# Forgetting attention's last gate products spread over the following units, its pooling splits moved behind them, and a cross-attention norm's sums moved to TensorE

## The reference, cut to what matters

```
z = rms_norm(x, mix_pre_g) @ w_in        # pool, q, k, v, forget logits, two gates of 1024 columns
y_pool = pool_mixer(u_pool, ...) @ w_pool_br
y_fox  = fox_attention(q, k, v, log_f) @ w_fox_br     # 8 heads, 8 query blocks of 128, causal
merged = sigmoid(z_gp) * y_pool + sigmoid(z_gf) * y_fox
x = x + rms_norm(merged @ w_mix_out, mix_post_g)
x = x + rms_norm(mem_attention(rms_norm(x, xa_pre_g), ...), xa_post_g)
h = rms_norm(x, ffn_pre_g)
x = x + rms_norm(conv_ffn(h, ...), ffn_post_g)
```

## Time and profile before

| what | us |
|---|---|
| median of 3 runs | 2921.78 (2920.51 to 2922.21) |
| the profiled execution, its own time | 2927.9 |
| its span, first to last instruction | 2926.0 |
| TensorE busy in it | 2823.0 (96%) |
| VectorE busy | 1270.6 (43%) |
| ScalarE busy | 795.1 (27%) |
| mean granted clock of TensorE | 0.984 |

### The profile page before, as it was taken

One profiled execution on the slowest core, in us unless ns is written; L12 is line 12 of the kernel. 1 busy time (PEld: TensorE's weight loads), 2 busy tenths in 40 slices (PEclk: granted clock), 3 DMA queues, 4 the chain that ended last, 5 costly groups with the idle time before them and its releaser, 6 DMA issues.

```text
span 2926.0 us, 35159 instructions
## 1 busy us (share of the span) xinstructions
PE 2823.0 (96%) x13916; PEld 2307.3 (79%) x13916; DVE 1270.6 (43%) x1788; ACT 795.1 (27%) x1234; POOL 970.0 (33%) x1008
## 2 busy tenths in 40 slices
PE   7999988999999999999999998999979999999998
PEld 6889876888888888878797776777658888888886
DVE  4266636543323223255204343458476343433436
ACT  5254426220001101143113333334452111111114
POOL 3622310743333333324332110364125333333330
PEclk9999999999999999999999999999989999999999
DMA  5423331311111111116543232432012111111103
GB/s 206 157 100 101 101 123 40 119 52 63 43 46 54 43 43 57 35 23 134 131 94 91 80 108 85 169 115 87 29 72 72 56 45 43 43 43 43 66 20 115
DMA packets 156934, 230.59 MB, mean 79 GB/s; under 512 B 5285, under 2 KB 116240, under 8 KB 156824
## 3 DMA queue, kind: packets, MB, share of 16 engines
q1 hardware_dynamic: 110448, 136.85, 16.2%
q10 hardware_dynamic: 46375, 92.24, 9.0%
HBM read 181.33 MB, written 47.74 MB: 78 GB/s over the span
## 4 chain that ended last, share of the span: by engine, by line
PE 84%; DVE 9%; ACT 3%; issue 2%; DMA 1%; ACTq 0%; POOL 0%; DVEq 0%; POOLq 0%
PE PS L906 30%; PE PS L297 22%; PE PS L919 10%; PE PS L1263 4%; PE PS L2313 3%; PE PS L1269 2%; PE PS L933 2%; PE PS L1320 2%; PE PS L1958 2%; PE PS L2028 1%; PE PS L2000 1%; PE PS L2016 1%; DVE SC L661 1%; DVE XT L1089 1%; DVE SC L1051 1%
## 5 line engine op out<-in xcount | busy, mean ns | idle before, releaser
L2942 POOL CAST wh<-raw 128x512 fp32r<-128x512 f32 (+1 forms) x488 | 336.6, 704 | 1870.4 <-issue 1185.8
L2946 POOL TENSOR_TENSOR wl<-raw,wh 128x512 fp32r<-128x512 f32 (+1 forms) x488 | 659.5, 1363 | 1.3 <-issue 1.3
L297 PE MATMUL PS<-UH,wh 128*128 128x512 f32 x1040 | 426.4, 410 | 10.6 <-DVE UL L2739 3.0
L297 PE MATMUL PS<-UH,wl 128*128 128x512 f32 x1040 | 407.9, 392 | 0.0
L297 PE MATMUL PS<-UL,wh 128*128 128x512 f32 x1040 | 407.7, 392 | 0.0
L906 PE MATMUL PS<-UL,wh 128*128 128x512 f32 x1280 | 394.1, 389 | 0.0
L906 PE MATMUL PS<-UH,wl 128*128 128x512 f32 x1280 | 394.0, 389 | 0.0
L906 PE MATMUL PS<-UH,wh 128*128 128x512 f32 x1280 | 393.9, 389 | 0.0
L906 PEld LDWEIGHTS PS<-UH,wl 128*128 128x128 f32 x1280 | 240.2, 188 | 50.0
L906 PEld LDWEIGHTS PS<-UL,wh 128*128 128x128 f32 x1280 | 240.2, 188 | 49.9
L906 PEld LDWEIGHTS PS<-UH,wh 128*128 128x128 f32 x1280 | 240.2, 188 | 49.8
(11 more groups left out here) (341 smaller groups left out, 3995.2 us busy)
## 6 DMA issues: line engine op xcount, KB each, us to landing
raw<-in_w_up SPq DMA_DIRECT2D x33, 1024.0 KB, 7.2
raw<-in_w_in SPq DMA_DIRECT2D x27, 1024.0 KB, 10.7
raw<-in_w_down SPq DMA_DIRECT2D x22, 1024.0 KB, 4.9
raw<-in_w_gate SPq DMA_DIRECT2D x11, 1024.0 KB, 5.3
raw<-in_w_out SPq DMA_DIRECT2D x8, 1024.0 KB, 6.1
xres<-XT ACTq DMA_DIRECT2D x4, 2048.0 KB, 7.3
zgate<-SC ACTq DMA_DIRECT2D x32, 256.0 KB, 2.0
SC<-zgate ACTq DMA_DIRECT2D x16, 512.0 KB, 4.4
```

The costliest lines, as they stand in the source:

```text
L297: mm = pe.matmul(PS[:, banks[f], :], w[:, k, f * P:(f + 1) * P], u[:, k, half(h)], start=(k == 0 and j == 0), stop=(k == n_k - 1 and j == 2))
L2942: pool.tensor_copy(wh[slot][:, cols], raw[slot % 2][:, cols]).then_inc(hi_done[slot], 1)
L2946: low = pool.tensor_tensor(wl[slot][:, cols], raw[slot % 2][:, cols], wh[slot][:, cols].bitcast(F32), ALU.subtract)
```

## The change

It has three parts. First, the gate products: up to step 26 all stays; the last 16 k-steps (tiles 30 and 31) are no longer made in steps 27 and 28 but four k-steps in each of steps 27 to 30, two at a time, each pair at one of three places (ahead of `turn`, behind it, behind `values`). ScalarE's copy of tile 30 moves to step 28 and that of tile 31 to step 30, both behind the exponentials. Second, the pooling splits: tile 0 in step 31, tiles 1 to 3 in step 32, where ScalarE does them ahead of unit 30's output; Branches' tile 0 waits for one low part per k instead of for all four. Third, phase 1 of half 0 of joined is summed on TensorE too: VectorE's seven `accumulate` go, the one `add_up` goes, and eight `total` products stand at four places between the last out tiles.

```diff
@@ HalfNorm
-                self.on_tensor, self.totals = on_tensor, counter("pooling_full", (KT - 1) * len(on_tensor))
+                self.on_tensor, self.totals = on_tensor, [counter(name, (KT - 1) * (len(on_tensor) > 0)) for name in ("pooling_full", "pooling_hi")]
...
-                    self.total(pe, 2 * k)
-                    self.total(pe, 2 * k + 1)
-
-            def total(self, pe, k):
-
-                pe.wait_ge(*self.sq[1](KT + k + 1))
-                mm = pe.matmul(PS[:, self.banks[1][1], :], ones[:], self.buf(k % 2, 1), start=k == 0, stop=k == KT - 1)
-                mm.then_inc(self.sums[1].sem if k == KT - 1 else self.totals.sem, 1)
+                    self.total(pe, 1, (2 * k, 2 * k + 1))
+
+            def total(self, pe, h, ks):
+
+                for k in ks:
+                    pe.wait_ge(*self.sq[h](KT + k + 1))
+                    mm = pe.matmul(PS[:, self.banks[h][1], :], ones[:], self.buf(k % 2, h), start=k == 0, stop=k == KT - 1)
+                    mm.then_inc(self.sums[h].sem if k == KT - 1 else self.totals[h].sem, 1)
...
-                    act.wait_ge(*(self.totals(k - 1) if (h, p) in self.on_tensor else self.acc[h](p * (KT - 1) + max(1, k - 2))))
+                    act.wait_ge(*(self.totals[h](k - 1) if (h, p) in self.on_tensor else self.acc[h](p * (KT - 1) + max(1, k - 2))))
@@ Second, TensorE
+                at = [self.AHEAD * KT]
+
+                def gates(n):
+
+                    for i in range(at[0], at[0] + n, 2):
+                        self.gate(pe, i // KT, range(i % KT, i % KT + 2))
+                    at[0] += n
+
                 for t in range(self.UNITS + 2):
-                    q = t + self.AHEAD
+                    first, second, third = (0, 4, 4) if t < 27 else {27: (2, 2, 0), 28: (2, 2, 0), 29: (0, 2, 2), 30: (2, 2, 0)}.get(t, (0, 0, 0))
                     if t < self.UNITS:
                         self.scores(pe, t)
+                    gates(first)
                     if t >= 2:
                         self.turn(pe, t - 2, (2, 3))
-                    if q < self.N_GATES:
-                        self.gate(pe, q, range(4))
+                    gates(second)
                     if t >= 2:
                         self.values(pe, t - 2)
-                    if q < self.N_GATES:
-                        self.gate(pe, q, range(4, KT))
+                    gates(third)
@@ Second, ScalarE
-                    q = t + self.AHEAD - 1
-                    if q < self.N_GATES:
-                        gate(q)
+                    if t < 28:
+                        gate(t + self.AHEAD - 1)
...
                         exponents(t)
+                    if t in (28, 30):
+                        gate(t // 2 + 16)
+                    if t == 31:
+                        act.wait_ge(*self.turned_loaded[0](16))
+                        act.wait_ge(*self.g_full(self.N_GATES))
+                    if t == self.UNITS:
+                        self.high(act, t)
                     if t >= 2:
                         output(t - 2)
+                    if t < self.UNITS:
+                        self.high(act, t)
...
-                    if t == 29:
-                        act.wait_ge(*self.turned_loaded[0](16))
-                        act.wait_ge(*self.g_full(self.N_GATES))
-                    for g in self.splits(t):
-                        act.activation(UH[:, g, :], XTf[:, g * T:(g + 1) * T], ACT.Copy).then_inc(self.hi.sem, 1)
...
-                return {29: (0,), 30: (1,), 31: (2, 3)}.get(t, ())
+                return {31: (0,), 32: (1, 2, 3)}.get(t, ())
+
+            def high(self, act, t):
+                for g in self.splits(t):
+                    act.activation(UH[:, g, :], XTf[:, g * T:(g + 1) * T], ACT.Copy).then_inc(self.hi.sem, 1)
@@ Branches
                     pe.wait_ge(*self.second.mx(32))
-                    pe.wait_ge(*self.second.lo(4))
...
                 for k in range(4):
+                    if n == 0:
+                        pe.wait_ge(*self.second.lo(k + 1))
@@ Chain, TensorE
+                self.joined.total(pe, 0, (0, 1))
                 for t in range(3):
                     self.out_tile(pe, KT + t, (3,))
+                self.joined.total(pe, 0, (2,))
                 for t in range(3, KT):
                     self.out_tile(pe, KT + t)
-                    if t == 4:
-                        self.joined.add_up(pe, 0, 1)
+                    self.joined.total(pe, 0, {3: (3, 4), 4: (5, 6, 7)}.get(t, ()))
@@ Chain, VectorE
-                        joined.renew(dve, 0, (k,))
+                        joined.renew(dve, 0, (k,), sums=False)
...
-                joined.renew(dve, 0, (6, 7))
+                joined.renew(dve, 0, (6, 7), sums=False)
@@
-                          store=True, on_tensor=((1, 1),))
+                          store=True, on_tensor=((0, 1), (1, 1)))
```

## The result

The changed kernel takes 2907.76 us in the median of five runs (2905.2 to 2908.28), the kernel before, in five runs on the same chip, 2921.78 (2920.51 to 2931.27). The ratio is 0.9941, with a 95% interval of 0.9930 to 0.9953: faster by 17.2 us (13.7 to 20.5), by the two medians alone by 14.0. The forecast was 2910.8, 11 us off.

The account below looks back on a forecast made before the run. TensorE was taken as the bound (84% of what ended last), so only its waits could be won: 6.0 us in the tail plus 5.0 in Chain, 11.0 off the 2921.8 median, giving 2910.8; range 2907 to 2916.

Parts of the forecast that it names:

- The path's rival: Tail of Second: added copies and k-steps count, missing splits don't; tail wins 1.6 to 2.5 us, 2914.8; chance 0.11.
- The totals' rival: Chain: totals and squares wait for each other; only 0 to 1.5 us won there, 2914.5 to 2916; chance 0.09.
- The rival that nothing is won in the tail: Tail: the reload's end is set by something absolute; part 3 alone counts, 2916.8; chance 0.07.
- the part on the clock: Steps 29 to 33: slow work hides in waits at no cost; 1.5 us kept in the range for tile 0.
- what follows the FFN's head only moves: Behind the FFN's head: nothing else is touched, so later code keeps its length and only shifts.
- everything behind a gain at 1842 moves with it: From the run of 288 products at 1842.22 on: the tail's gain, taken as 6.0 us, passes on whole.
- Tail: Steps 27 on to tile 4 of Branches, parts 1 and 2: 6.0 us won, bounds 1.6 to 8.3.
- Middle: Untouched code from tile 4 of Branches to TensorE's 3.0 us wait in Chain: forecast 0.
- Chain piece: End of Chain to the FFN head's last low-part wait, part 3: sum complete at 2147.0 against 2152.0, 5.0 us won.
- My bound of 6.5: Part 3 in Chain: upper bound of its gain, 6.5 us, if the clock and the lock fall well.
- the larger gain: Whole kernel: a gain larger than the forecast band of 2907.5 to 2914; chance 0.02.
- a reason for a slower kernel: Steps 31 to 33, tiles 0 to 3: products strewn between waits keep 1.2 GHz; +8 us, 2929.8; half-clock rival, chance 0.03.

Follow-up runs that it names:

- e1: The changed kernel without part 3 (gate products, splits and single waits only; half 0's sums stay on VectorE): 2913.38 us, ratio 0.9970 to the kernel before.
- e11: The kernel before with 22 useless products in the waits of steps 30 to 32 and the sums on TensorE (part 3): 2917.61 us, ratio 0.9980.
- e10: The kernel before, unchanged, run once more for a second trace: 2921.81 us in one execution.
- e4: The changed kernel with the gate products back at before's places, late splits, single waits and totals kept: 2911.14 us, ratio 0.9966 to the kernel before.
- e13: The kernel before with 12 useless products ahead of tile 3's in Branches, before the wait for tile 4: 2922.09 us against 2923.82, ratio 0.9994.
- e7: The changed kernel with unit 31's first transposes ahead of Branches' tile 0 and its values inside tile 0: 2904.74 us, ratio 0.9932 to the kernel before.
- e8: e7 plus gate tile 31's copy a step later, all high parts in step 32, half 1's squares added one k earlier: 2902.62 us, ratio 0.9924.
- e12: e8 with 12 useless products in TensorE's 3.0 us wait in Chain: 2902.18 us, ratio 0.9929 to the kernel before.
- e2: The kernel before with part 3 alone (half 0's sums on TensorE): 2920.87 us, ratio 0.9993 to the kernel before.
- e9: e2 unchanged, run again (part 3 alone on the kernel before): 2919.18 us against 2923.28, ratio 0.9986.
- e14: The changed kernel with 12 useless products in TensorE's 3.0 us wait in Chain: 2909.31 us, ratio 0.9953 to the kernel before.
- e6: The kernel before with 22 useless products put into TensorE's waits of steps 30 to 32: 2919.50 us against 2922.09, ratio 0.9986.

## Why the prediction was right and where it failed

**Right, in sign and mechanism.** Both halves of the change win, each in the waits that it was aimed at; no rival happened. Unit 29's scores came 5.6 us earlier (5.5 worked out), tile 4 kept its wait (2.85 us), the single waits cost nothing, one wait for all costs 2.75 us (3 worked out), and the totals have no wait. The path's rival is out: tail -7.3 us, not -2. The totals' rival is out: the distances between the four groups of totals are 3.80, 3.62 and 4.49 us where I had 3.8, 3.6 and 4.4. The rival that nothing is won in the tail is out by e1.

**The step that failed** stands in the part on the clock: "the slow work lies inside the waits, and costs the path nothing", together with "what follows the FFN's head only moves" and "everything behind a gain at 1842 moves with it". The prediction allowed 1.5 us for slow products in the changed kernel's tile 0, and did not see that before's tile 0 had them already: in the earlier trace rows unit 30's values at 1813.03 take 1.98 us, and from there to unit 31's values, with one wait of 0.47 in between, the trace takes 9.16 us where the same products take 7.68 at full clock (e11). I compared two orders worked out at full clock, and took what before's trace has beyond its order for something that both kernels share. Three terms were mis-sized by it:

- Tail: -6.0 forecast, -7.3 in the two pairs of traces (380.3 to 382.4 us in the four with before's tail, 372.8 to 374.3 in the four with the new one). At full clock on both sides the forecast holds: 379.0 (e11) against 372.8, 6.2 us, and from unit 29's scores to unit 30's values 21.2 us (e10, e11) against 20.7, the 0.5 that I took. What comes on top is before's half clock: 1.4 to 2.7 us between unit 30's and unit 31's values in each trace with its tail, and 0.7 ahead of them in three of these five; so its two traces average 1.6 over 379.0, the two of the changed kernel 0.6 over 372.8, and 6.2 + 1.6 - 0.6 are the 7.3 but for rounding. The worked order itself was a little long in its waits: 6.1 us in six where the changed kernel's trace has 4.4 in four. The account of the parts was also wrong. I had 5.5 for the gate products and 0.5 for the path; e4 shows 4.4 for the late splits with their single waits and 2.9 for the gates on top, 1.6 of it the clock. The two overlap, since both empty the same waits.
- Middle: 0 forecast, -2.5. The half clock behind the wait for tile 4 costs 67.17 - 65.56 = 1.6 us in the run of 288; without that wait (e13, e7, e8, e12) the run takes 65.6 us in all four traces. The rest of the middle is 214.3 to 214.7 us in before, e10, e2, e9 and e11, and 212.8 to 213.1 in eight of the eleven others of the table (211.3 in e13, 214.6 in e8 and e14), again steps of 1.6. But this is a matter of frequency and not of certainty: the second trace of the changed kernel takes 67.19 us there too. That before's waits in the tail make the slow place behind tile 4 likelier is what the counts suggest (four of four against four of eight); with so few traces that can be chance, and a cause is not shown.
- Chain piece: -5.0 forecast, -6.3. The groups of totals keep their distances; the first group stands 6.84 us behind the wait's end where I had 8.24 (2132.3 - 2124.06). I had taken the products ahead of it from before's trace. In e2, e9, the changed kernel and e14 the same distance is 8.08, 6.73, 6.84 and 5.29: it goes down in steps of about 1.4 us as less of it runs at the half clock, and with the wait filled it is shortest. Where it is as long as before's, in e2, the piece is 44.5 and the gain 5.1, as forecast; the rest goes with the half clock getting shorter there. My bound of 6.5 for this case held it.

By the sum of the three, 16 us; by the medians 14.0 and 14.6; by the ratio 17.2. The forecast of 11 is 3 to 6 us short, and that much lies in these terms. How much of it one execution draws is luck; that before's tail runs slow behind its last waits is seen in all five traces of it. By the medians the time still lies in the band that I had called the forecast (2907.5 to 2914), by the ratio in the larger gain, to which I had given 0.02.

The Trainium skill, in the page TensorE: Matmul & The Clock Gate, section on the HAM clock gate, says that how many matmuls run cold at a kernel's start varies from run to run of one kernel, with the phase of a free-running observation. The traces agree as far as the scatter goes, here in mid-kernel: waits of 2.9 us before equal products, with the clock at 0.70 or at 1.00 behind them. The phase itself no run here shows. What the Trainium skill says in the same page's section on psum-queue depth-cycling, which I weighed as a reason for a slower kernel, agrees with before's 0.74 among its waits; but the changed kernel, with four waits left, held 1.00 in one execution and 0.76 at one place in the other.

## What to carry to other kernels

Count a wait on TensorE as more than its length: here 2.75 us of waiting cost 5.0 in one place, and the wait of 3 us ahead of tile 4 was followed by 1.4 to 2.8 us of loss in eight traces of twelve. Look for half-clock products behind the last wait, where nothing hides them: before's tail had 1.5 us of them in the very rows that were read. When an order worked out at full clock is ahead of the trace, the gap is a term of its own that the change may remove, and not a constant to subtract from both sides. And test two parts of a change apart before sharing the gain between them: spread products and late splits emptied the same waits, and on paper I had given nearly all of it to the one that brought less.

## What the runs showed of the hardware that I had not expected

- The same instructions ahead of line 1958 took 1453 to 1464 us in different executions and kernels, with a granted clock of 0.99 in that stretch in every trace. One trace cannot place a gain of 3 us; cuts at common instructions can.
- Useless products in a wait can shorten what lies behind it: e13's run of 288 by 1.6 us, e14's Chain piece by 1.6 us. Neither was a gain that the medians could tell in the whole kernel; e6's 2.6 us is at the edge (ratio 0.9996 at the upper end). They can also miss the place that counts: in e6 the waits had the clock back, and unit 30's values and tile 0 did not.
- The run of 288 products at tile 4 has a sharp lowest value, 65.55 to 65.58 us in eight traces, and otherwise mostly 67.17 to 67.19 (six traces).
